# The first two units of a streamed trunk step divided at 256 tokens, and the first norm's root taken in token columns

## The chip, the core and the metric

One core of a Trainium2 chip runs the program. The metric is the device time of one execution in microseconds. All times in the profile are microseconds from the start of the span unless marked ns. The engines are TensorE (PE), VectorE (DVE), ScalarE (ACT), GpSimd (POOL) and SyncE (SP), which issues most DMAs; each executes its own list of instructions in order and waits on semaphores.

## What is computed

One layer of a hybrid trunk for 512 prompt tokens and 32 sample tokens, with all weights shared. Only the first half-step FFN and its norm are touched:

```
def rms_norm(x, g):
    y = xf * lax.rsqrt(jnp.mean(xf * xf, axis=-1, keepdims=True) + EPS)
    return (y * g.astype(jnp.float32)).astype(x.dtype)
def swiglu(x, wg, wu, wd):
    return (jax.nn.silu(x @ wg) * (x @ wu)) @ wd
# trunk_layer:
x = x + 0.5 * swiglu(rms_norm(x, g_ffn1), w_ffn1_gate, w_ffn1_up, w_ffn1_down)
... # mixer (mLSTM and retention), second half-step FFN
y_prompt = rms_norm(hp, g_final)
```

D_MODEL is 1024, D_FF 2816. Everything is float32.

## The kernel before

The 544 tokens (T) are kept as columns: x is turned to xT, 8 k-tiles (DT) of 128 features by 544 tokens. The token chunks are 0 to 3 of 128 tokens each, and the sample chunk, index NC = 4, of 32. A **unit** is one product of 128 output features with all tokens; units 0 and 1 are gate and up of the first 128 features of D_FF, units 2 and 3 of the next, and so on. Each product runs in a split form: weights and inputs are each divided into a rounded part (w_hi, xg_hi) and a rest (w_lo, xg_lo), and three of the four combinations are summed in PSUM: hi by hi ("hh"), hi by lo ("hl"), lo by hi ("lh"). A matmul takes TH = 272 columns, so a unit is 8 k-tiles x 3 parts x 2 halves = 48 matmuls.

At the start SyncE loads x chunk by chunk (x_tok, token rows) and the first weights (w_raw); the weights of unit 0 come in two halves of four k-tiles. TensorE first turns 12 dummies, then x (L848, L840) and the gains (L836) into PSUM. dense[0] and dense[1] hold one chunk each, so chunks 2 and 3 wait until 0 and 1 are copied out. VectorE copies most pieces to xT (L1779, L1782), ScalarE two of them (L1267). ScalarE makes xg_hi = gain times xT, 544 columns for each k-tile (L1042), and w_hi (L1272, L1284, L1030); VectorE makes xg_lo (L1424) and w_lo (L1784, L1790, L1419). The norm is not applied to xg but later, to the product: its factor rstd is multiplied in when a unit is evicted from PSUM (L1678, L1685).

For rstd, ScalarE squares x by token rows with a sum along the row (L1255, x_sums, one column for each chunk); GpSimd writes each sum on the diagonal of a block of sq_sum (L2065); TensorE multiplies it by a matrix of ones (L626, norm_sums_of), which puts each token's sum in its column on all partitions. In unit 1, behind its k-tile 5, these matmuls stand (SUMS_K). ScalarE takes the root over 544 columns (L1047) and VectorE the reciprocal (L1430).

The order of everything is the order in which each engine's part is written. The functions that matter are first_product (unit 0), second_product (unit 1) and plain (all other units of this kind) on TensorE, plain and the code ahead of ffn(0, 0) on ScalarE and VectorE, and spread_sums on GpSimd. Unit 2 needs w_lo of its own (w_lo_ready) and no eviction, since it writes to other banks; unit 3 needs unit 0 evicted, unit 4 unit 1.

## Time and profile before

| | us |
|---|---|
| median of 3 runs (1066.98 to 1067.19) | 1067.0 |
| the profiled execution | 1067.28 |
| its span, first to last instruction | 1065.5 |
| TensorE busy | 1055.8 (99%) |
| VectorE busy | 686.1 (64%) |
| ScalarE busy | 467.6 (44%) |
| GpSimd busy | 191.2 (18%) |

The profile is of one execution. The 1.8 us between its time and its span lie around the program. A share of busy time is an average; what a change is worth is read at the place where it is made, from what waits there and for whom. A matmul's record is longer than the step to the next, since they are pipelined: a row of n matmuls that takes t has steps of (t - one) / (n - 1). A releaser in brackets is inferred from the semaphores.

### The profile page before, as it was taken

Reading aid. Unit: us, or ns where it says so; the run is one execution under the profiler, and the core shown is the slowest. Engines: PE = TensorE matmul, PEld = TensorE weight load, DVE = VectorE, ACT = ScalarE, POOL = GpSimd, SP = SyncE. Lnnn points to the kernel's source line nnn. Section 1 sums busy time; section 2 is a strip of 40 time slices with the busy share of each in tenths; the row PEclk is TensorE's granted clock in tenths of the full one; section 3 lists DMA queues with packets and bytes.
Section 4 is the critical chain, followed back from the end, with each engine's and each line's share of the span. In section 5 each row is a group of like instructions: output and inputs, shape, how many; then the busy total and the mean of one; then the engine's idle time right before and its main releaser. Section 6 shows DMA issues by size and latency. Waiting matters only on the chain.

```text
span 1065.5 us, 20471 instructions
## 1 busy us (share of the span) xinstructions
PE 1055.8 (99%) x8424; PEld 1052.3 (99%) x8424; DVE 686.1 (64%) x1161; ACT 467.6 (44%) x820; POOL 191.2 (18%) x168
## 2 busy tenths in 40 slices
PE   8999999999999999999999999999999999999997
PEld 8999999999999999999999999999999999999997
DVE  5998752357766676555655556598875236777555
ACT  7466641246663335433222224446664114666323
POOL 1122100012201211210332222212210002220111
PEclk9999999999999999999999999999999999999999
DMA  7489572388833377445454224547958338882422
GB/s 224 90 185 203 112 183 84 102 161 175 175 83 92 72 131 144 70 69 79 72 80 73 68 78 61 140 91 170 205 109 187 91 90 163 177 176 55 120 75 84
DMA packets 245350, 127.84 MB, mean 120 GB/s; under 512 B 9181, under 2 KB 243717, under 8 KB 245129
## 3 DMA queue, kind: packets, MB, share of 16 engines
q1 hardware_dynamic: 206888, 106.79, 41.4%
q0 software_dynamic: 38288, 19.72, 14.6%
q8 instruction: 67, 1.10, 0.4%
q14 instruction: 27, 0.21, 0.1%
q10 hardware_dynamic: 80, 0.02, 0.0%
HBM read 123.22 MB, written 3.29 MB: 119 GB/s over the span
## 4 chain that ended last, share of the span: by engine, by line
PE 98%; DMA 1%; DVE 0%; ACT 0%; SPq 0%; issue 0%; ACTq 0%
PE dense L589 52%; PE dense L737 30%; PE core_banks L737 5%; PE core_banks L589 3%; PE core_banks L890 1%; PE core_banks L905 1%; PE dense L793 1%; PE core_banks L908 1%; PE core_banks L880 1%; DMA x_tok<-in_x_prompt 1%; PE dense L646 1%; PE dense L659 1%; PE core_banks L874 0%; PE core_banks L917 0%; PE core_banks L876 0%; PE core_banks L774 0%
## 5 line engine op out<-in xcount | busy, mean ns | idle before, releaser
L1419 DVE TENSOR_TENSOR w_lo<-w_raw,w_hi 128x1024 fp32r<-128x1024 f32 (+2 forms) x119 | 132.8, 1134 | 55.1 <-ACT w_hi L1030 55.0
L1030 ACT ACTIVATE w_hi<-w_raw 128x1024 fp32r<-128x1024 f32 (+2 forms) x119 | 106.3, 906 | 89.2 <-PE dense L589 81.0
L589 PE MATMUL dense<-h_hi,w_hi 128*128 128x272 f32 x684 | 142.4, 290 | 0.0
L589 PE MATMUL dense<-xg_hi,w_hi 128*128 128x272 f32 x672 | 142.2, 293 | 0.0
L589 PE MATMUL dense<-h_lo,w_hi 128*128 128x272 f32 x684 | 141.2, 287 | 0.0
L589 PE MATMUL dense<-h_hi,w_lo 128*128 128x272 f32 x684 | 140.9, 287 | 0.0
L589 PE MATMUL dense<-xg_lo,w_hi 128*128 128x272 f32 x672 | 138.9, 288 | 0.0
L589 PE MATMUL dense<-xg_hi,w_lo 128*128 128x272 f32 x672 | 138.8, 288 | 0.0
L737 PE MATMUL dense<-x_op_hi,w_lo 128*128 128x272 f32 x432 | 124.6, 289 | 0.0
L737 PE MATMUL dense<-x_op_hi,w_hi 128*128 128x272 f32 x432 | 124.5, 288 | 0.0
L737 PE MATMUL dense<-x_late_hi,w_lo 128*128 128x272 f32 x432 | 124.5, 288 | 0.0
L737 PE MATMUL dense<-x_late_hi,w_hi 128*128 128x272 f32 x432 | 124.3, 288 | 0.0
L737 PE MATMUL dense<-x_late_lo,w_hi 128*128 128x272 f32 x432 | 124.2, 287 | 0.0
L737 PE MATMUL dense<-x_op_lo,w_hi 128*128 128x272 f32 x432 | 124.0, 287 | 0.0
L1476 DVE TENSOR_TENSOR w_lo<-w_src,w_hi 128x512 fp32r<-128x512 f32 x126 | 85.8, 689 | 50.0 <-ACT w_hi L1078 49.8
L1733 DVE SCALAR_TENSOR_TENSOR xT<-dense,xT 128x544 f32<-128x544 f32 x38 | 27.5, 724 | 135.4 <-PE dense L589 135.3
L589 PEld LDWEIGHTS dense<-h_lo,w_hi 128*128 128x128 f32 x684 | 107.9, 188 | 0.0
L589 PEld LDWEIGHTS dense<-h_hi,w_lo 128*128 128x128 f32 x684 | 106.8, 188 | 0.0
L589 PEld LDWEIGHTS dense<-h_hi,w_hi 128*128 128x128 f32 x684 | 106.7, 188 | 0.1
L589 PEld LDWEIGHTS dense<-xg_lo,w_hi 128*128 128x128 f32 x672 | 105.8, 188 | 0.0
L589 PEld LDWEIGHTS dense<-xg_hi,w_lo 128*128 128x128 f32 x672 | 105.1, 188 | 0.0
L589 PEld LDWEIGHTS dense<-xg_hi,w_hi 128*128 128x128 f32 x672 | 104.7, 188 | 0.2
(333 smaller groups left out, 2217.3 us busy)
## 6 DMA issues: line engine op xcount, KB each, us to landing
w_src<-in_w_ffn_gate SPq DMA_DIRECT2D x90, 256.0 KB, 4.8
w_raw<-in_w_ffn_up SPq DMA_DIRECT2D x90, 256.0 KB, 3.9
w_raw<-in_w_in SPq DMA_DIRECT2D x32, 512.0 KB, 8.9
w_raw<-in_w_ffn_down SPq DMA_DIRECT2D x32, 384.0 KB, 4.1
w_raw<-in_w_ffn_down SPq DMA_DIRECT2D x32, 320.0 KB, 3.5
w_src<-in_w_ffn_gate POOLq DMA_DIRECT2D x36, 256.0 KB, 5.4
w_raw<-in_w_ffn_up POOLq DMA_DIRECT2D x36, 256.0 KB, 5.8
w_raw<-in_w_ffn_up SPq DMA_DIRECT2D x8, 512.0 KB, 5.0
```

Source lines behind the costliest of these rows:

```text
L589: last = nc.tensor.matmul(out[:, half, 0:TH], w[:, s % 4, k, :], x(kt)[:, half * TH:(half + 1) * TH], start=start and n == 0 and m == 0, s ...
L646: last = nc.tensor.matmul(bank_of(0)[:, half, 0:TH], w[:, 0, k, :], x(k)[:, half * TH:(half + 1) * TH], start=m == 0, stop=m == len(order) ...
L659: last = nc.tensor.matmul(bank_of(1)[:, half, 0:TH], w[:, 1, k, :], part(k)[:, half * TH:(half + 1) * TH], start=w is w_hi and k == 0 and ...
L737: last = nc.tensor.matmul(banks[BANK[o]], w[:, k, :], x[:, k, :], start=o in OPENS and k == 0 and m == 0, stop=k == KH - 1 and m == 2, ski ...
L793: last = nc.tensor.matmul(bank_of(t)[:, part, 0:cols.stop - cols.start], w[:, (s + u) % 4, kt - u * split, :], x[:, kt, cols], start=kt == ...
L880: nc.tensor.matmul(X[:, 3, CH[c]], p(h, 1, CH[c]), p(h, 0, CH[c]), start=True, stop=True)
L890: last = nc.tensor.matmul(X[:, b, o * V1:(o + 1) * V1], k_tail[:, c, :], v_tok[:, c, :], start=True, stop=True)
L905: last = nc.tensor.matmul(out, score_tail[:, block], v_tok[:, c, :], start=True, stop=c == 0)
L1030: nc.scalar.activation(w_hi[:, s % 4, 0:k_tiles(s), :], raw, ACT.Copy).then_inc(w_hi_ready, 1)
L1419: nc.vector.tensor_tensor(w_lo[:, s % 4, 0:nk, :], w_raw[:, s % RAW, 0:nk, :], w_hi[:, s % 4, 0:nk, :].bitcast(F32), ALU.subtract).then_in ...
L1476: nc.vector.tensor_tensor(block_of(w_lo, n, o), source(p % 2, o), block_of(w_hi, n, o).bitcast(F32), ALU.subtract)\
L1733: nc.vector.scalar_tensor_tensor(x, halves(tile), factor, x, ALU.mult, ALU.add).then_inc(evicted, 1)
```

## The change

- Units 0 and 1 are divided by tokens into EARLY (256, chunks 0 and 1) and LATE (288, chunks 2, 3 and the sample). first_units replaces first_product and second_product: unit 0 early, with the turns of the sample, chunk 2 and half of chunk 3 set between its products; unit 1 early (hh and hl), the last half of chunk 3, unit 1 early lh; then the late tokens of both units side by side. The matmuls have 256 and 288 columns. Both units are done at the same moment.
- Chunks 2 and 3 and the sample are turned into other PSUM banks (x_home) and no longer wait for dense. The eight dummies before the first product are gone.
- xg_hi and xg_lo of units 0 and 1 are made in 8 early and 8 late pieces. Unit 1's weights too come in two halves, unit 0's first half moves up to the third place in SyncE's list, before the sample.
- The first norm: GpSimd makes rstd itself, in one column for each chunk (mean and eps, then a power of -0.5), before it writes it on the diagonal. TensorE's matmuls then yield rstd in columns, and ScalarE only copies it. Reciprocal and root over 544 columns go. ScalarE squares chunks 0 and 1 ahead of the first product, the sample and chunk 2 behind the late pieces; VectorE squares chunk 3. The matmuls with ones move from unit 1 to unit 2, behind two of its k-tiles.

In the diff, cut to its core:

```diff
-    X_BY_ACT = [(2, 1), (3, 1)]
+    X_BY_ACT = [(2, 0), (2, 1)]
+    NA = 2 * P
+    EARLY, LATE = slice(0, NA), slice(NA, T)
...
+        def x_home(c, half):
+            if c < 2:
+                return dense[c][:, half, :]
+            if c == 2:
+                return X[:, half, :]
+            if c == NC:
+                return X[:, 2, 0:DT * TS]
+            return X[:, 3, :] if half == 0 else X[:, 0, :]
...
             load_x(0)
             load_x(1)
+            load_half(0, w_ffn1_gate, 0)
             load_x(NC)
             load_x(2)
+            load_half(0, w_ffn1_gate, 1)
             load_x(3)
+            load_half(1, w_ffn1_up, 0)
+            load_half(1, w_ffn1_up, 1)
...
-            SUMS_K = (5, 5, 6)
+            SUMS_K = (2, 5, 6)
...
+            def first_units():
+
+                order = [("hh", 0)]
+                for k in range(1, DT):
+                    order += [("hh", k), ("lh", k - 1), ("hl", k - 1)]
+                order += [("lh", DT - 1), ("hl", DT - 1)]
                 for m, (part, k) in enumerate(order):
+                    first_part(0, part, k, False, m == 0, m == len(order) - 1)
+                    if (part, k) == ("hl", 2):
+                        for piece in ((NC, 0), (2, 0), (2, 1)):
+                            turn_x(*piece)
+                    if (part, k) == ("hl", 4):
+                        turn_x(3, 0)
+                pe.wait_ge(x_taken, 4)
+                for k in range(DT):
+                    for part in ("hh", "hl"):
+                        first_part(1, part, k, False, part == "hh" and k == 0, False)
+                turn_x(3, 1)
+                for k in range(DT):
+                    first_part(1, "lh", k, False, False, k == DT - 1)
+                for m, (part, k) in enumerate(order):
+                    for u in range(2):
+                        last = first_part(u, part, k, True, m == 0, m == len(order) - 1)
...
-            turn_dummies(KEEP_WARM)
...
+                if n == 0:
+
+                    nc.scalar.activation(rstd[:, :].rearrange("p (a b) -> p a b", a=2), X[:, 0:2, 0:TH], ACT.Copy).then_inc(rstd_ready, 1)
+                    return
...
+                link(nc.gpsimd.tensor_scalar(col, x_sums[0:r, c:c + 1], 1.0 / D, EPS, ALU.mult, ALU.add))
+                link(nc.gpsimd.tensor_tensor(col, col, minus_half[0:r, c:c + 1], ALU.pow))
+                nc.gpsimd.tensor_scalar(sq_sum[0:r, CH[c]], ident[0:r, 0:r], col, None, ALU.mult).then_inc(x_sums_spread, 1)
+
+            for n, c in enumerate((0, 1, NC, NC - 1, 2)):
+                spread_rstd(n, c)
```

How instructions stand in a row, at three places. TensorE, from the turns of the sample on (dense0 and dense1 are the banks of units 0 and 1; core_banks, in the code X, are four others). Before:

```order
L840 MATMUL core_banks<-sum_ident,x_tok 128x32 x7
L836 MATMUL core_banks<-sum_ident,gain_rows 128x40 [waits gains_loaded]
L848 MATMUL dense<-sum_ident,x_tok 128x128 [waits x_taken,x_loaded2]
...
L848 MATMUL dense<-sum_ident,x_tok 128x128 [waits x_taken,x_end_loaded]
L848 MATMUL dense<-sum_ident,x_tok 128x128 x3
L829 MATMUL core_banks<-sum_ident 128x128 x8
L646 MATMUL dense<-xg_hi,w_hi 128x272 [waits half_hi,xg_hi_ready,x_taken_act,x_taken]
```

Now, from the gains on:

```order
L884 MATMUL core_banks<-sum_ident,gain_rows 128x40 [waits gains_loaded]
L668 MATMUL dense<-xg_hi,w_hi 128x256 [waits early_hi,half_hi0] x2
...
L668 MATMUL dense<-xg_lo,w_hi 128x256 [waits early_lo,half_hi0]
L873 MATMUL core_banks<-sum_ident,x_tok 128x32 [waits x_loaded4]
L873 MATMUL core_banks<-sum_ident,x_tok 128x32 x7
L877 MATMUL core_banks<-sum_ident,x_tok 128x128 [waits x_loaded2]
...
L668 MATMUL dense<-xg_lo,w_hi 128x256 [waits early_lo,w_hi_ready]
L877 MATMUL core_banks<-sum_ident,x_tok 128x128 [waits x_taken_act,x_end_loaded]
L877 MATMUL core_banks<-sum_ident,x_tok 128x128 x3
L668 MATMUL dense<-xg_hi,w_lo 128x256 [waits early_hi,half_lo1] x4
```

The first products stand ahead of the turns of the sample, and the last half of chunk 3 stands behind 40 of them.

ScalarE, from the gains to unit 2's weights. Before:

```order
L1261 ACTIVATE gains<-core_banks 128x40 [waits gains_moved]
L1267 ACTIVATE xT<-dense 128x4x128 [waits x_moved]
L1272 ACTIVATE w_hi<-w_raw 128x512 [waits half_loaded]
L1042 ACTIVATE xg_hi<-xT,gains 128x544 [waits gains_ready,x_taken]
...
L1030 ACTIVATE w_hi<-w_raw 128x1024 [waits w_loaded1]
L1255 ACTIVATE x_squared,x_sums<-x_tok 128x1024 [waits x_summed,x_end_loaded,x_loaded3]
L1030 ACTIVATE w_hi<-w_raw 128x1024 [waits w_loaded2]
```

Now:

```order
L1300 ACTIVATE w_hi<-w_raw 128x512 [waits half_loaded0]
L1313 ACTIVATE gains<-core_banks 128x40 [waits gains_moved]
L1317 ACTIVATE xg_hi<-xT,gains 128x256 [waits x_taken,gains_ready]
...
L1306 ACTIVATE xT<-core_banks 128x4x128 [waits x_moved] x2
L1328 ACTIVATE xg_hi<-xT,gains 128x288 [waits x_taken_act,x_taken] x8
L1063 ACTIVATE w_hi<-w_raw 128x1024 [waits w_loaded2]
L1294 ACTIVATE x_squared,x_sums<-x_tok 32x1024 [waits x_summed,x_loaded4]
L1294 ACTIVATE x_squared,x_sums<-x_tok 128x1024 [waits x_summed,x_loaded2]
L1063 ACTIVATE w_hi<-w_raw 128x1024 [waits w_loaded3]
```

Two squares now stand behind the late pieces and behind unit 2's weights.

GpSimd, behind its constants, the first chunk. Before:

```order
L2061 MEMSET sum_ident 128x544
L2065 TENSOR_SCALAR sum_ident<-sum_ident,x_sums 128x128 [waits x_summed,pool_step]
```

Now:

```order
L2138 MEMSET minus_half 128x5 [waits pool_step]
L2147 TENSOR_SCALAR x_rstd<-x_sums 128x1 [waits x_summed,pool_step]
L2148 TENSOR_TENSOR x_rstd<-x_rstd,minus_half 128x1 [waits pool_step]
L2149 TENSOR_SCALAR sum_ident<-sum_ident,x_rstd 128x128 [waits pool_step]
```

One operation for each chunk has become three, each waiting for the one before (pool_step); the five chunks follow each other so.

## Rows read from the trace of the kernel before

**Rows 1.** The page: the chain that ended last, share of the span by engine.
```profile
PE 98%; DMA 1%; DVE 0%; ACT 0%; SPq 0%; issue 0%; ACTq 0%
```
**Rows 2.** Waits of TensorE: who waited for whom, us in total, times, longest.
```profile
PE dense L804 <- ACT rms_bias L1220: 0.9, 1, 0.9
PE dense L848 <- DMA x_tok<-in_x_prompt: 0.6, 1, 0.6
PE dense L646 <- ACT xg_hi L1042: 0.4, 1, 0.4
```
**Rows 3.** Timeline of TensorE, start: start us, us, engine line op, xcount [idle before].
```profile
1.90 2.82 PE L829 MATMUL core_banks<-sum_ident 128*128 128x128 f32 x12 [1.90 <-POOL eps L2028]
...
7.35 0.68 PE L840 MATMUL core_banks<-sum_ident,x_tok 32*128 32x32 f32 x8
7.96 0.25 PE L836 MATMUL core_banks<-sum_ident,gain_rows 40*128 40x40 f32 x1
...
11.22 1.04 PE L829 MATMUL core_banks<-sum_ident 128*128 128x128 f32 x8
12.30 0.49 PE L646 MATMUL dense<-xg_hi,w_hi 128*128 128x272 f32 x2
...
13.43 0.49 PE L646 MATMUL dense<-xg_hi,w_hi 128*128 128x272 f32 x2 [0.39 <-ACT xg_hi L1042]
```
**Rows 4.** Timeline of TensorE, units 1 and 2, and the first matmul of unit 3.
```profile
22.31 0.41 PE L659 MATMUL dense<-xg_lo,w_hi 128*128 128x272 f32 x2
...
23.73 0.41 PE L659 MATMUL dense<-xg_lo,w_hi 128*128 128x272 f32 x2
...
24.48 2.17 PE L659 MATMUL dense<-xg_hi,w_lo 128*128 128x272 f32 x16
26.49 0.41 PE L589 MATMUL core_banks<-xg_hi,w_hi 128*128 128x272 f32 x2
...
32.52 0.29 PE L589 MATMUL dense<-xg_hi,w_hi 128*128 128x272 f32 x1
```
**Rows 5.** Timeline of ScalarE, 7 to 21 us.
```profile
7.14 1.06 ACT L1255 ACTIVATE x_squared<-x_tok 32x1024 f32<-32x1024 f32 x1
...
8.38 1.06 ACT L1255 ACTIVATE x_squared<-x_tok 128x1024 f32<-128x1024 f32 x1
...
10.00 0.63 ACT L1272 ACTIVATE w_hi<-w_raw 128x512 fp32r<-128x512 f32 x1
...
12.54 2.02 ACT L1042 ACTIVATE xg_hi<-xT,gains 128x544 fp32r<-128x544 f32 x3
...
19.54 1.04 ACT L1030 ACTIVATE w_hi<-w_raw 128x1024 fp32r<-128x1024 f32 x1
```
**Rows 6.** Timeline of VectorE, 6 to 16 us.
```profile
6.46 1.89 DVE L1779 COPY xT<-dense 128x512 f32<-128x512 f32 x3 [0.16 <-PE dense L848]
...
13.31 2.18 DVE L1424 SCALAR_TENSOR_TENSOR xg_lo<-xT,gains,xg_hi 128x544 fp32r<-128x544 f32 x3 [0.34 <-ACT xg_hi L1042]
```
**Rows 7.** DMA issues at 1.73, 2.19 and 4.83 us: xcount, KB each, us to landing.
```profile
x_tok<-in_x_sample SPq DMA_DIRECT2D x1, 128.0 KB, 4.7
...
x_tok<-in_x_prompt SPq DMA_DIRECT2D x1, 512.0 KB, 6.1
...
w_raw<-in_w_ffn_up SPq DMA_DIRECT2D x1, 512.0 KB, 8.6
```
**Rows 8.** Single lines L1042 and L1216 of ScalarE: xcount, ns min/median/max, first and last start.
```profile
L1042 ACT ACTIVATE xg_hi<-xT,gains x24: 734/750/755, 11.4 to 682.5; 128x544 fp32r<-128x544 f32 x24
...
L1216 ACT ACTIVATE x_gain<-xT,gains x2: 508/523/538, 1053.8 to 1058.4; 128x288 f32<-128x288 f32 x1, 128x256 f32<-128x256 f32 x1
```
**Rows 9.** GpSimd: its line L2065, its power L2112, and two small forms (xcount | busy, mean ns).
```profile
L2065 POOL TENSOR_SCALAR sum_ident<-sum_ident,x_sums x5: 354/605/770, 6.0 to 19.7; 128x128 f32<-128x128 f32 x4, 32x32 f32<-32x32 f32 x1
...
L2112 POOL TENSOR_TENSOR small<-small x8: 1168/1180/1202, 437.4 to 639.8; 128x5 f32<-128x5 f32 x8
...
L2106 POOL TENSOR_TENSOR sum_ident<-proj,table 128x32 f32<-128x32 f32 x4 | 1.0, 247 | 0.0
...
L2028 POOL MEMSET eps<- 128x1 f32 x1 | 0.1, 99 | 0.0
```

More of the change, by code:

```diff
@@ L650, in second_product, with first_part @@
[L650 to L663 removed]
+            def first_part(u, part, k, late, start, stop):
+                w, x = {"hh": (w_hi, xg[0]), "hl": (w_hi, xg[1]), "lh": (w_lo, xg[0])}[part]
+                half, cols = (1, LATE) if late else (0, EARLY)
+                if part == "lh":
+                    if k < DT // 2:
+                        pe.wait_ge(half_lo[u], 1)
+                    else:
+                        pe.wait_ge(w_lo_ready, u + 1)
+                elif k < DT // 2:
+                    pe.wait_ge(half_hi[u], 1)
+                else:
+                    pe.wait_ge(w_hi_ready, u + 1)
+                if part == "hl":
+                    pe.wait_ge(xg_lo_ready if late else early_lo, k + 1)
+                else:
+                    pe.wait_ge(xg_hi_ready if late else early_hi, k + 1)
+                a = 0 if late else 512 - NA
+                return nc.tensor.matmul(bank_of(u)[:, half, a:a + cols.stop - cols.start], w[:, u, k, :], x(k)[:, cols],
+                                        start=start, stop=stop)
@@ L1285, in _ @@
-            split_hi(0, 1, 0)
-            square_x(NC, NC - 1)
+            act.wait_ge(gains_ready, 1)
+            for j in range(DT):
+                act.wait_ge(x_taken, X_BY_DVE.index((1, 2 * j // DT)) + 1)
+                nc.scalar.activation(xg_hi[:, j, EARLY], xT[:, j, EARLY], ACT.Copy, scale=gains[:, G_FFN1 + j:G_FFN1 + j + 1])\
+                    .then_inc(early_hi, 1)
+                if j == DT // 2 - 1:
+                    half_to_hi(0, 1)
+            half_to_hi(1, 0)
+            half_to_hi(1, 1)
@@ L1288, in _ @@
+            for c, half in X_BY_ACT:
+                take_x(c, half)
+            for j in range(DT):
+                act.wait_ge(x_taken, X_BY_DVE.index((3, 2 * j // DT)) + 1)
+                act.wait_ge(x_taken_act, X_BY_ACT.index((2, 2 * j // DT)) + 1)
+                nc.scalar.activation(xg_hi[:, j, LATE], xT[:, j, LATE], ACT.Copy, scale=gains[:, G_FFN1 + j:G_FFN1 + j + 1])\
+                    .then_inc(xg_hi_ready, 1)
             ffn(0, 0)
@@ L1792, in _, with half_to_lo @@
-            split_lo(0, 1, 0)
+                    out, tiles = xT[:, :, CH[c]], x_home(c, half).rearrange("p (k d) -> p k d", d=TS)
+                nc.vector.tensor_copy(out, tiles).then_inc(x_taken, 1)
+            def half_to_lo(u, half):
+                k = slice(half * DT // 2, (half + 1) * DT // 2)
+                if half:
+                    dve.wait_ge(w_hi_ready, u + 1)
+                else:
+                    dve.wait_ge(half_hi[u], 1)
+                nc.vector.tensor_tensor(w_lo[:, u, k, :], w_raw[:, u, k, :], w_hi[:, u, k, :].bitcast(F32), ALU.subtract)\
+                    .then_inc(w_lo_ready if half else half_lo[u], 1)
@@ new lines, in part_lo @@
+            def part_lo(j, cols, hi_ready, lo_ready):
+                dve.wait_ge(hi_ready, j + 1)
+                nc.vector.scalar_tensor_tensor(xg_lo[:, j, cols], xT[:, j, cols], gains[:, G_FFN1 + j:G_FFN1 + j + 1],
+                                               xg_hi[:, j, cols].bitcast(F32), ALU.mult, ALU.subtract).then_inc(lo_ready, 1)
+            for c in range(2):
+                for half in range(2):
+                    take_x(c, half)
+            for j in range(DT):
+                if 2 * j % DT == 0:
+                    half_to_lo(0, 2 * j // DT)
+                part_lo(j, EARLY, early_hi, early_lo)
```

199 lines of the change are left out of this document (88 added, 111 removed).

## Prediction

> **What bounds the kernel now.** I read the page's chain first: TensorE carries 98% of it [rows 1]. Past the wait before its first instruction, the list of waits has three of TensorE: 0.6 for a piece of x, 0.4 for a piece of xg_hi, 0.9 in the tail [rows 2]. So what the change can move is what happens before TensorE's stream closes; from there on each microsecond saved or lost goes to the end unchanged. I then read TensorE's timeline of the start [rows 3]. Behind the turns of chunks 0 and 1 the sample rows are turned at 7.35, the gains at 7.96, then chunks 2 and 3 as their DMAs land; eight dummy transposes fill from 11.22; the first product starts at 12.30, and at 13.43 the second k-tile of xg_hi lets it go on. The two first units are through at 26.49, when unit 2 begins, and unit 3 begins at 32.52 [rows 4]. Within that, the norm's sums cost 0.92: from the pair of products at 22.31 to the one at 23.73 are 1.42, less two pairs at 0.25.
>
> **The sum is made at the start of unit 3**, because the norm's sums move from unit 1 into unit 2. Before: 32.52. Without its sums the first pair of units would have ended at 26.49 - 0.92 = 25.57.
>
> **When the first product starts now.** Chunks 0 and 1 are turned and copied as before: VectorE's fourth copy ends at 6.46 + 1.89 = 8.35 [rows 6]. ScalarE needs the gains before it can scale. They are turned on TensorE right behind chunk 1, where the sample rows began at 7.35, and no longer behind these, at 7.96 [rows 3]. No row says when their DMA landed, so these are the bounds; I take 7.7, the middle. ScalarE meanwhile does two squares, 1.24 from one to the next (7.14 to 8.38), and the first half of w_hi (0.63) [rows 5], whose DMA is now third instead of fifth in the queue: 1.25 MB into the stream, where the sample rows (1.125 MB) landed 4.7 us after issue at 1.73, that is 6.4, and chunk 2 (1.625 MB) at 2.19 + 6.1 = 8.3 [rows 7]. By that scale it lands at 6.9, ScalarE is through by 7.6. Gains: 7.7 + 0.25 for the turn, 0.18 for the copy, some 0.1 of hand-overs: 8.2. The first early piece of xg_hi is 256 columns wide, a form that the trace has: 508 ns [rows 8]. End 8.73, and TensorE starts 0.14 after such an end (13.43, after ScalarE's piece begun at 12.54, of three in 2.02, so 0.75 long and 0.64 a step [rows 5]). First product: **8.87**, bounds 8.5 and 9.15.
>
> **What TensorE does from there to unit 2.** The same columns as before in as many products, cut otherwise: 48 of 256 columns and 48 of 288 where 96 had 272. Those run 0.1253 apart (the row of 16 begun at 24.48: (2.17 - 0.29) / 15 [rows 4]); by columns that is 0.118 and 0.133, and the 96 keep their 12.03: cutting is free. Turning moves in between: 16 turns at (1.04 - 0.27) / 7 = 0.110, as the dummies', are 1.75, and the sample rows 0.70 [rows 3]. In the first groups the pieces come at ScalarE's and VectorE's pace (some 0.41 each for 256 columns: the 0.64 a step less 288 columns at (750 - 508) / 288 = 0.84 ns), and TensorE asks for three products, 0.35, per piece: three small waits of 0.2 in all, and 0.35 where a group's first matmul follows a wait (0.20 to the second in place of 0.125, as at 13.43). Weight halves come in time: w_hi's second at 9.95 + 0.6, those of unit 1 when 2.875 and 3.125 MB are in (12.5 and 13.4; the whole landed at 4.83 + 8.6 = 13.4 before), split by 14.1 [rows 5, 7], and TensorE is at unit 1 at 14.3. If a weight half were 0.5 late, that cover would be gone and it would cost about that. Sum: 8.87 + 12.03 + 2.45 + 0.55 = 23.9, **23.95** with its last matmul's hand-over, for the start of unit 2: 1.6 earlier than 25.57. Removing the eight dummies costs nothing by itself: they stood in a wait.
>
> **The norm's sums are what is late next.** They stand after two of unit 2's eight k-tiles: 12 matmuls, so TensorE asks for all five diagonal blocks at 23.95 + 1.50 = 25.45, and as its queue is in order, everything behind waits: 36 more products of unit 2 and all that follows. What must be done by then:
> - TensorE reaches the last piece of chunk 3 only behind unit 1's 16 products: 8.87 + 0.55 + 40 x 0.118 + 2.0 of turns = 16.15. It ends its four turns at 16.85, and VectorE has copied it by 17.5 (1.89 for three such copies, some 0.65 [rows 6]).
> - ScalarE's late pieces 4 to 7 wait for that copy. A 288-column piece takes 538 ns [rows 8], 0.44 a step, so the four steps end at 19.3. Then it splits w_hi of unit 2 (1.04), to 20.3, squares the sample rows, to 21.5, and chunk 2, to 22.7 (1.24 each) [rows 5]. The order rows in the section on the change show this row of instructions; before, these two squares lay ahead of the first product.
> - VectorE: eight late lo pieces to 21.0 (0.44 a step: three of 544 columns took 2.18, 0.70 a step [rows 6], less 256 columns at 1.0 ns, its time per column by the same row), then chunk 3's square over 1024 columns, some 1.2: 22.2. Unit 2's w_lo, as many columns, then ends at 23.3, ahead of 23.95 by 0.65. The reciprocal of the first norm leaves VectorE and brings nothing: TensorE did not wait for it [rows 2].
> - GpSimd now does three operations for each chunk in place of one, and chunks sample, 3 and 2 still lie ahead of it at 21.5. The wide one is 354 to 770 ns by its row; I take 0.35 for the sample and 0.77 for the others, the latest and longest of the five [rows 9]. The scale and shift of one column: between a 128x1 memset, 0.10, and the 32x32 form, 0.354; I take 0.27. The power of one column: the nearest row is the power of 128x5, 1.18 us; the nearest without a power is a product of 128x32, 0.247. If the 0.93 between them is work per column, one column costs 0.25 + 0.19 = 0.44. Three self-waits are some 0.06 each. The chain is then 21.5 + 1.26 = 22.76, + 1.66 = 24.4, + 1.66 = **26.1**, 0.15 more to TensorE: it starts the sums at 26.25, 0.8 late.
>
> **Sum.** -1.6 + 0.8 = -0.8 at the start of unit 3 (31.7). Behind it I see nothing that becomes late: the root's copy and the first eviction, each some 0.75 for 544 columns [rows 5, 6], need some 1.7 us with hand-overs, and TensorE has 4.5 us of unit 2 left; the second eviction has 6 us more. The table load before the root goes; the one for the silu stays behind the copy, off TensorE's path. The profiled execution would have a span of 1064.7 and, with the 1.8 around it, 1066.5; that run stood 0.3 above the median of 1067.0, so the forecast is 1067.0 - 0.8 = **1066.2**.
>
> What a page says of this, outside the sum: the Trainium skill, "GPSIMD Engine Reference", section "Elementwise — side-by-side cycle accounting", counts about 2.6 cycles per element and a dispatch for each instruction, so a power of one column would cost little more than the start of an instruction. The row [rows 9] speaks against taking that for powers: five columns cost 1.18 us where 32 columns of a product cost 0.247. By the page's rule the stall would be 0.2 and the time 1065.6.
>
> **The rivals.**
> - *The power has a fixed price (slower).* If one column costs what five cost, 1.18, the three powers in a row add 3 x 0.74 = 2.2 to the chain: blocks ready at 28.3, TensorE idle for 3.0, net +1.4: 1068.4. The point is a power of 0.71: 0.8 of gain is then eaten. For it: the row is the only power in the trace, and its eight instances lie within 3%. Against: a product of 544 columns on GpSimd takes far longer than one of 32, so its operations are counted per column.
> - *No stall at the sums.* With 0.25 for the power and 0.10 for the scale the blocks are ready at 25.0: the whole 1.6 stays, 1065.4; with the gains' DMA at its early bound, 1065.0.
> - *TensorE's pace falls back.* The granted clock reads 1.00 from the start, yet the first twelve transposes stand 0.218 apart ((2.82 - 0.42) / 11) and the later dummies 0.110 [rows 3]: half the pace, in TensorE's first microseconds.  Now it is nearly idle from 7.3 to 8.9 with no dummies behind. If it came back for some 4.4 us (the dummies' 2.6 and as much of chunk 0), 2.2 us would be lost: +1.4, 1068.4. Against it: it is 1.6 us of idling, and the trace has waits of 0.6 and 0.4 [rows 2] with no loss of pace behind them. "TensorE: Matmul & The Clock Gate" of the Trainium skill, section "Part 1: The HAM clock gate (the "warmup" mystery)", says that half pace is the default and that an idle engine returns to it; by it the price would be the same.
> - *The change does not fill the gap.* The early tokens come no sooner if the gains or the first weight half land later than I scaled; 0.5 later moves the whole start by 0.5 and leaves 1066.7, inside the main case.
>
> **How the numbers follow.** Main case (power near 0.44, stall 0.3 to 1.3) 0.50, 1065.7 to 1066.9; fixed price 0.22; no stall 0.15; pace 0.05; the rest 0.08, of it half each way. The range reaches from the no-stall case with early gains, 1065.0, to the fixed-price case, 1068.5. A difference of 0.2%, 2.1 us, is about what a measurement of this kernel can tell from none. Faster by more would need over 2.1 of the 3 us that lay open before the first product, without any stall: 0.05. Slower by more needs the fixed price and the pace together, or a late DMA on top of one: 0.06. Within: 0.89.
>
> **What would show it.** In the profile after: the first product of 256 columns near 8.9; unit 2's first near 23.9; an idle of TensorE just before the sums' matmuls, released by GpSimd, of about 0.8; one power on GpSimd near 0.44. A power near 1.2, or transposes 0.21 apart after 8 us, would name the rival. No wait at all and a gain of 1.6 would mean the small operations are cheaper than I hold. Wrong altogether if unit 3 waits for the first eviction, or if TensorE waits at unit 2 for w_lo.

## The result, and the profile after

The change made the kernel slower. The median went from 1066.99 us (6 runs, 1066.8 to 1067.35) to 1072.18 us (6 runs, 1071.37 to 1075.63), a ratio of 1.0048 with a 95% interval of 1.0034 to 1.0062. The profiled run of after took 1071.62 us with a span of 1069.9, against 1067.28 and 1065.5 before: 4.4 us more between the first and the last instruction. Three runs far off all others (one at 1280 us in experiment 9, and two of before beside it, at 1134 and 2130) count in no comparison below.

All of it is there when unit 3 begins, at 36.86 us against 32.52 [rows 4], 4.34 later. Four views show from where. First the waits of TensorE in the profile after (who waited for whom, us in total, times, longest), to be read against [rows 2]:

```profile
PE core_banks L647 <- POOL sum_ident L2149: 2.7, 1, 2.7
...
PE dense L668 <- ACT xg_hi L1317: 0.9, 1, 0.9
...
PE core_banks L884 <- DMA gain_rows<-in_g_gn_ret: 0.5, 1, 0.5
```

The wait for GpSimd at the norm's sums was forecast, at 0.8. It is 2.7. Then TensorE's timeline (start us, us, what, xcount, [idle before]), which answers to [rows 3, 4]:

```profile
7.70 0.25 PE L884 MATMUL core_banks<-sum_ident,gain_rows 40*128 40x40 f32 x1 [0.54 <-DMA gain_rows<-in_g_gn_ret]
8.89 0.83 PE L668 MATMUL dense<-xg_hi,w_hi 128*128 128x256 f32 x2 [0.94 <-ACT xg_hi L1317]
...
10.02 0.41 PE L668 MATMUL dense<-xg_hi,w_hi 128*128 128x256 f32 x1
10.23 0.41 PE L668 MATMUL dense<-xg_hi,w_lo 128*128 128x256 f32 x1
10.44 0.41 PE L668 MATMUL dense<-xg_lo,w_hi 128*128 128x256 f32 x1
...
12.42 1.97 PE L877 MATMUL core_banks<-sum_ident,x_tok 128*128 128x128 f32 x8
...
16.64 0.28 PE L668 MATMUL dense<-xg_hi,w_hi 128*128 128x256 f32 x1
16.76 0.28 PE L668 MATMUL dense<-xg_hi,w_lo 128*128 128x256 f32 x1
...
26.90 0.42 PE L616 MATMUL core_banks<-xg_hi,w_hi 128*128 128x272 f32 x2
...
28.16 0.42 PE L616 MATMUL core_banks<-xg_hi,w_lo 128*128 128x272 f32 x2
31.31 1.19 PE L647 MATMUL core_banks<-sum_ident,ones 128*128 128x272 f32 x4 [2.73 <-POOL sum_ident L2149]
...
36.86 0.41 PE L616 MATMUL dense<-xg_hi,w_hi 128*128 128x272 f32 x2
```

The first product starts at 8.89, in place of 12.30. But from there to 16 us the products of 256 columns start 0.21 apart (10.02, 10.23, 10.44) and eight turns take 1.97, where behind 16.6 us the same products are 0.12 apart. TensorE's granted clock in stretches of 2 us (the columns are the stretch, busy time and instructions of PE, its weight loads, VectorE, ScalarE and GpSimd, then the granted clock, the DMA share and GB/s) says the same:

```profile
8.00:10.00 2.00, 1.06 (x4) 0.92 (x5) 2.00 (x5) 1.97 (x7) 1.22 (x2) 0.86 1.07 349
10.00:12.00 2.00, 2.00 (x14) 1.78 (x12) 2.00 (x6) 2.00 (x5) 0.00 (x0) 0.50 1.15 309
12.00:14.00 2.00, 2.00 (x13) 1.94 (x13) 1.11 (x3) 1.72 (x4) 0.00 (x0) 0.50 1.19 291
14.00:16.00 2.00, 2.00 (x11) 2.00 (x10) 0.00 (x0) 0.76 (x2) 0.00 (x0) 0.50 1.07 224
16.00:18.00 2.00, 2.00 (x18) 2.00 (x17) 1.51 (x3) 0.78 (x2) 0.00 (x0) 0.94 0.75 193
```

0.50 is the lower of the two levels, 1.2 GHz in place of 2.4. It lasts from 9.5 to 16.3 us, and it begins after TensorE stood idle for 0.54 and 0.94 us with one transpose between. In before every such stretch up to 36 us reads 1.00. Unit 2 therefore starts at 26.90 and not at the forecast 23.95. "TensorE: Matmul & The Clock Gate" of the Trainium skill, section "Part 1: The HAM clock gate (the "warmup" mystery)", names the lower level as the engine's default when idle. The trace agrees on the two levels, and shows the fall behind two idle stretches as short as 0.54 and 0.94 us.

The other part is GpSimd's chain. Its timeline, with one power of chunk 1 first, then the three operations for the sample and those for chunk 3, and under it VectorE's timeline over the same time:

```profile
7.92 0.58 POOL L2148 TENSOR_TENSOR x_rstd<-x_rstd,minus_half 128x1 f32<-128x1 f32 x1
...
24.39 0.68 POOL L2147 TENSOR_SCALAR x_rstd<-x_sums 32x1 f32<-32x1 f32 x1 [15.08 <-ACT x_squared L1294]
25.16 1.44 POOL L2148 TENSOR_TENSOR x_rstd<-x_rstd,minus_half 32x1 f32<-32x1 f32 x1
26.70 1.29 POOL L2149 TENSOR_SCALAR sum_ident<-sum_ident,x_rstd 32x32 f32<-32x32 f32 x1
28.08 0.19 POOL L2147 TENSOR_SCALAR x_rstd<-x_sums 128x1 f32<-128x1 f32 x1
28.35 0.57 POOL L2148 TENSOR_TENSOR x_rstd<-x_rstd,minus_half 128x1 f32<-128x1 f32 x1
29.02 0.61 POOL L2149 TENSOR_SCALAR sum_ident<-sum_ident,x_rstd 128x128 f32<-128x128 f32 x1
```

```profile
23.82 1.22 DVE L1867 SCALAR_TENSOR_TENSOR x_squared_dve<-x_tok 128x1024 f32<-128x1024 f32 x1
...
24.96 1.22 DVE L1462 TENSOR_TENSOR w_lo<-w_raw,w_hi 128x1024 fp32r<-128x1024 f32 x1
26.54 1.23 DVE L1462 TENSOR_TENSOR w_lo<-w_raw,w_hi 128x1024 fp32r<-128x1024 f32 x1 [0.36 <-ACT w_hi L1063]
```

The smallest of the five blocks is the slowest: 0.68, 1.44 and 1.29 us on 32 partitions, where the larger chunk 3 takes 0.19, 0.57 and 0.61. Each of the three slow ones ends just behind a VectorE instruction that was already running when it started: the first at 25.07 (VectorE's square ends at 25.04), the power at 26.60 (the first w_lo ends at 26.18), the scaling at 27.99 (the second ends at 27.77). Behind the last w_lo, VectorE is idle and GpSimd is quick.

### The profile page after: what moved, and what is told of

Read it like the earlier page. It is cut to its first block, busy times and chain, and to the rows that moved or that the text cites. A ratio compares the mean times of both kernels' runs of the same rounds, so it can differ in the third digit from the quotient of the medians.

```text
span 1069.9 us, 20574 instructions
## 1 busy us (share of the span) xinstructions
PE 1057.2 (99%) x8416; PEld 1054.2 (99%) x8416; DVE 685.0 (64%) x1171; ACT 467.1 (44%) x826; POOL 197.2 (18%) x179
## 4 chain that ended last, share of the span: by engine, by line
PE 97%; POOL 1%; ACT 1%; DMA 1%; DVE 0%; issue 0%; SPq 0%; ACTq 0%
PE dense L616 52%; PE dense L766 30%; PE core_banks L766 5%; PE core_banks L616 3%; PE core_banks L923 1%; PE core_banks L938 1%; PE dense L822 1%; PE core_banks L941 1%; PE core_banks L913 1%; PE dense L668 1%; DMA w_raw<-in_w_ffn_gate 1%; PE core_banks L950 0%; PE core_banks L909 0%; PE core_banks L907 0%; PE core_banks L647 0%; PE core_banks L877 0%
```

## The experiments

All edits are on after, except where before is named. Each set of experiments (1 to 4; 5 to 8; 9 and 10) had runs of before beside it, whose median was 1067.17, 1067.0 and 1067.03. Mean clocks are those of a whole run; half pace for 6.8 of 1065 us takes 0.003 off them.

**1. Fill TensorE's idle time.** Is it half pace that puts unit 2 three us late?

```diff
+            turn_dummies(5)
             pe.wait_ge(gains_loaded, 16 * 6)
             nc.tensor.transpose(X[:, 3, 0:5 * DT], gain_rows[:, :], ...)
+            turn_dummies(8)
             ffn(0, 0)
```

> The kernel after with 13 more dummy transposes of TensorE: 5 ahead of the gains' turn and 8 behind it, where it stood idle from 7.2 to 7.7 and from 7.95 to 8.9. Theory: two things ate the gain, TensorE's half pace from 9.3 to 16.1 us (products of 256 columns 0.213 apart instead of 0.118), which came after that idling, and the wait of 2.7 us before the norm's sums. Then the half pace is gone: products 0.118 apart from the first on, unit 2 at 23.95 as predicted instead of 26.90, the wait before the sums as long as it was (ScalarE's squares and GpSimd's blocks move with TensorE), time 1072.2 - 2.9 = 1069.3. Rival: the half pace comes from the mixture of short products and turns with their waits, not from the idling; then it stays and so does 1072.2.

Measured: median 1069.3 (1068.67 to 1072.31, 6 runs), ratio to before 1.0026 (1.0015 to 1.0038): the forecast value. Every stretch from 8 to 28 us reads 1.00, unit 2 starts at 24.80. That is 0.85 behind the expectation, as the first product is (9.74), for two reasons: chunk 1's turns ended later, and the five dummies ahead of the gains' turn then stood in no wait, so that they delayed it by some 0.5 themselves (experiment 5, with as late a chunk 1 and no dummies, has 9.07). The profiled run was the slowest, 1072.31, and shows why: half pace now came later, behind the wait at the sums. In the views of TensorE's timeline and of the stretches:

```profile
29.19 2.18 PE L647 MATMUL core_banks<-sum_ident,ones 128*128 128x272 f32 x4 [2.71 <-POOL sum_ident L2151]
```

```profile
28.00:30.00 2.00, 0.81 (x2) 0.69 (x3) 0.00 (x0) 0.00 (x0) 1.04 (x2) 0.60 1.06 305
30.00:32.00 2.00, 2.00 (x8) 1.64 (x7) 0.00 (x0) 0.59 (x1) 0.00 (x0) 0.50 1.09 282
```

So the dummies take half pace out of the start, and the wait at the sums can bring it back. Of the six runs four lie at 1068.7 to 1069.4 and two above 1071.

**2. Ask for the sums later**, behind six k-tiles of unit 2.

```diff
-            SUMS_K = (2, 5, 6)
+            SUMS_K = (6, 5, 6)
```

> The kernel after with the matmuls of the norm's sums behind six of unit 2's eight k-tiles instead of two (24 matmuls, 3.0 us later in TensorE's order). Theory: the wait of 2.7 to 2.9 us before the sums is one for GpSimd's blocks, which come when they come; TensorE works 3.0 us of unit 2 meanwhile, so the wait goes but for 0.1, and what is left of unit 2 (12 matmuls, 1.5 us) just covers root copy and eviction: 1072.2 - 2.8 = 1069.4. Rival: the wait only moves to unit 3, which then waits for unit 0's eviction: over 1071. The half pace at the start stays in both.

Measured: median 1072.1 (1068.31 to 1072.98, 7 runs), ratio 1.0036 (1.0022 to 1.005). The wait at the sums is gone (they start at 32.28, the last block was ready at 32.09), and the median is that of after. In the profiled run the first product came 0.8 later than in after, because the first weight half landed later. Behind unit 3, which starts at 34.92, two waits on VectorE and ScalarE stand that after does not have. The timeline of TensorE:

```profile
9.72 0.76 PE L668 MATMUL dense<-xg_hi,w_hi 128*128 128x256 f32 x2 [1.71 <-ACT xg_hi L1317]
...
41.60 0.52 PE L616 MATMUL dense<-xg_hi,w_hi 128*128 128x272 f32 x2 [0.41 <-DVE w_lo L1462]
...
70.27 0.39 PE L766 MATMUL dense<-x_op_hi,w_hi 128*128 128x272 f32 x1 [1.28 <-ACT kept L1136]
```

With steps of 0.125 as normal, the step to 41.60 (0.70) loses 0.6, that to 70.27 (1.56) loses 1.4, and one at 34.92 (0.34) loses 0.2: 2.2 in all. After has no such step behind 32.5. So of the 2.7 us 2.2 were given back, and the late first product took more than the rest. That the later root is what made ScalarE and VectorE late is my reading of the order; no run tests it. Two of the seven runs, at 1068.31 and 1068.63, have mean clocks of 0.999 and 0.998 against 0.994 to 0.996 of four others: without half pace the kernel lies just below the 1068.7 to 1069.4 of experiment 1, which again leaves a gain of some 0.5 of the 2.7. (The seventh, 1072.98 at 0.999, is not explained.) My expectation, 1069.4, missed the new waits.

**3. Square earlier.** ScalarE's squares of the sample and of chunk 2 go between its late pieces 3 and 4, where it waited for chunk 3; VectorE's square of chunk 3 goes ahead of the last copy of x.

```diff
-                        square_x(2, NC)
-                        square_x(3, 2)
...
             for j in range(DT):
+                if j == DT // 2:
+                    square_x(2, NC)
+                    square_x(3, 2)
...
             half_to_lo(1, 1)
-            take_x(3, 1)
-            for j in range(DT):
-                part_lo(j, LATE, xg_hi_ready, xg_lo_ready)
...
+            take_x(3, 1)
+            for j in range(DT):
+                part_lo(j, LATE, xg_hi_ready, xg_lo_ready)
```

> The kernel after with the three late squares moved ahead: ScalarE's of the sample rows and of chunk 2 into its idle time between late pieces 3 and 4, VectorE's of chunk 3 into its idle time ahead of the copy of the last half of chunk 3. Theory: the blocks are then ready before TensorE asks for them at 28.4, the wait is gone, and the late pieces of xg_hi lose nothing since TensorE is at unit 1's early products: 1072.2 - 2.9 = 1069.3. Rival: the late pieces 4 to 7 slip by up to 1.0 and TensorE waits for them: 1070.3 or more. Also tells why GpSimd's first chain took 0.68, 1.44 and 1.29 us where the next took 0.19, 0.57 and 0.61: if VectorE's split of weights beside it is the cause, the sample's chain is short now; if the first chain after a long idle time is slow by itself, it is as long as before.

Measured: median 1068.16 (1065.32 to 1070.01, 10 runs), ratio 1.0006 (0.9994 to 1.0017). The wait at the sums is gone, although the profiled run (1069.82) has half pace from 10.5 to 17.3 us, as long as after has. The four runs at 1065.3 to 1065.9, with mean clocks of 0.998 and 0.999, are below every run of before; the six at 1067.5 to 1070.0 have 0.994 to 0.997. In the profiled run the gains landed late, so that the first product came 1.3 later than in after:

```profile
9.03 0.25 PE L884 MATMUL core_banks<-sum_ident,gain_rows 40*128 40x40 f32 x1 [1.35 <-DMA gain_rows<-in_g_gn_ret]
10.21 0.95 PE L668 MATMUL dense<-xg_hi,w_hi 128*128 128x256 f32 x2 [0.92 <-ACT xg_hi L1315]
```

GpSimd's timeline and VectorE's, here with other neighbours:

```profile
21.64 0.56 POOL L2149 TENSOR_TENSOR x_rstd<-x_rstd,minus_half 32x1 f32<-32x1 f32 x1
22.30 0.50 POOL L2150 TENSOR_SCALAR sum_ident<-sum_ident,x_rstd 32x32 f32<-32x32 f32 x1
...
26.59 1.43 POOL L2149 TENSOR_TENSOR x_rstd<-x_rstd,minus_half 128x1 f32<-128x1 f32 x1
```

```profile
25.23 2.36 DVE L1463 TENSOR_TENSOR w_lo<-w_raw,w_hi 128x1024 fp32r<-128x1024 f32 x2
```

The sample's power is quick now, 0.56, and that of chunk 2, beside w_lo, takes 1.43. So neither 32 partitions nor being the first after a long idle makes an operation slow; the company of VectorE does. The edit moves all three squares at once, so what each is worth was not told apart.

**4. Before, without its eight dummies**, for the prediction's statement that removing them costs nothing.

```diff
-            turn_dummies(KEEP_WARM)
             ffn(0, 0)
```

> The kernel before without its eight dummy transposes between the turns of x and the first product (11.2 to 12.3 us). Theory: the dummies are what kept TensorE's pace there; without them idle time from 11.4 to 12.3 and at 13.0 brings the half pace back for about as long as in the kernel after, 6.8 us, which costs 3: 1070. Rival: the idle time of 0.9 us is too short to matter, everything is as before: 1067.0.

Measured: median 1066.94 (1066.79 to 1070.15, 10 runs), ratio 1.0003 (0.9994 to 1.0013). TensorE then idles for 0.92 us before its first product at 11.97, and the profiled run stays at full clock. Eight of the ten runs lie within 1066.8 to 1067.6; two, at 1069.7 and 1070.15, have the size of a loss that half pace brings, but their mean clock is 0.999, where after's six runs have 0.992 to 0.996. So half pace does not show in them, and what cost the 3 us stays open.

**5. Hold one w_lo of VectorE** until GpSimd is through, to test the standing side by side alone.

```diff
                     if n == 0 and u == 0:
+                        dve.wait_ge(x_sums_spread, NC + 1)
                         split_lo(0, s + 3, 0)
```

> After, with one wait more: VectorE's split of unit 3's w_lo (1.22 us, begun at 26.54) waits until GpSimd has written all five blocks. Unit 2's split, begun at 24.96, stays. Theory (GpSimd and VectorE exclude one another during such an instruction): the sample's scaling on GpSimd, which took 1.29 beside that split, takes about 0.6, while its power beside unit 2's split stays at 1.44; the blocks are ready 0.7 earlier, the wait at the sums is 2.0 in place of 2.7, the time 1071.5. Rival (first operations after a long idle, or operations on 32 partitions, are slow by themselves): scaling stays at 1.29, wait 2.7, 1072.2.

Measured: median 1069.77 (1067.75 to 1073.24, 7 runs), ratio 1.0032 (1.0019 to 1.0044). GpSimd's timeline, the sample's power and scaling and the last scaling, and the first product and the wait at the sums on TensorE's:

```profile
25.61 1.44 POOL L2149 TENSOR_TENSOR x_rstd<-x_rstd,minus_half 32x1 f32<-32x1 f32 x1
27.14 0.36 POOL L2150 TENSOR_SCALAR sum_ident<-sum_ident,x_rstd 32x32 f32<-32x32 f32 x1
...
30.16 0.61 POOL L2150 TENSOR_SCALAR sum_ident<-sum_ident,x_rstd 128x128 f32<-128x128 f32 x1
```

```profile
9.07 0.76 PE L668 MATMUL dense<-xg_hi,w_hi 128*128 128x256 f32 x2 [0.93 <-ACT xg_hi L1317]
...
30.82 1.49 PE L647 MATMUL core_banks<-sum_ident,ones 128*128 128x272 f32 x4 [1.78 <-POOL sum_ident L2150]
```

The one operation whose neighbour was taken away fell from 1.29 to 0.36; the one beside the w_lo that stayed kept its 1.44. From the chain's first start to its last end it is 5.93 (24.84 to 30.77) in place of 6.86 (24.39 to 31.25), and the wait went from 2.73 to 1.78. That settles the cause of the long chain: VectorE's company, and neither the 32 partitions nor the idle time ahead. This profiled run had only one idle stretch at its start, 0.93 before the first product at 9.07, and fell to 0.50 all the same, from 11.1 us. In the medians the clock's scatter is larger than the effect tested, so the verdict rests on the rows.

**6. Dummies and squares together**, the diffs of 1 and 3 in one kernel.

> After with both edits of the earlier runs: five dummy turns ahead of the gains' and eight behind it, and the squares moved forward (ScalarE's sample and chunk 2 between late pieces 3 and 4, VectorE's chunk 3 ahead of the last copy of x). Theory (two causes, half pace after the start and a late chain on GpSimd): the run with squares moved gave 1065.3 to 1065.9 where its clock did not fall, so now every run should stand there, 1065.5 in the median, with unit 2 at 24.3 to 24.9 us, no half pace before 30 us and a wait at the sums under 0.7. Rival (TensorE comes early and GpSimd does not follow, since its chain starts behind ScalarE's squares and VectorE's splits whatever the clock is): a wait at the sums of over 1.5 and 1067 or more, and half pace behind that wait in some runs.

Measured: median 1066.2 (1065.39 to 1071.16, 11 runs), ratio 0.9994 (0.9986 to 1.0003). Ten of the eleven runs lie at 1065.4 to 1066.5, one at 1071.2. The profile has no wait at the sums and no clock below 1.00 up to 36 us:

```profile
8.86 0.76 PE L668 MATMUL dense<-xg_hi,w_hi 128*128 128x256 f32 x2
...
23.92 0.42 PE L616 MATMUL core_banks<-xg_hi,w_hi 128*128 128x272 f32 x2
...
25.43 1.08 PE L647 MATMUL core_banks<-sum_ident,ones 128*128 128x272 f32 x4
...
30.86 0.41 PE L616 MATMUL dense<-xg_hi,w_hi 128*128 128x272 f32 x2
```

Unit 3 starts at 30.86, 1.66 before that of before, and the span is 1063.9, 1.6 shorter. The last block was ready at 24.77, so 0.66 was to spare. Against before the medians alone do not settle a gain, since the interval holds 1.0; that the start is 1.66 shorter rests on the rows.

**7. The same, and unit 3's w_lo held** as in 5.

> As the kernel with both edits, and VectorE's split of unit 3's w_lo waits for all five blocks of rstd from GpSimd. Theory (a GpSimd operation stands still until VectorE's subtraction of two SBUF operands ends): the last operations on GpSimd take their 0.19, 0.57 and 0.61 and the blocks are ready up to 1.0 us earlier than without the hold; the time is equal or up to 0.7 lower, 1065.0 to 1065.5. Rival (GpSimd is slow for a reason of its own): no operation of it gets shorter, same time. If unit 3's weights then come late for unit 3, a wait of TensorE for w_lo appears at about 31 us and the time is higher.

Measured: median 1065.76 (1065.37 to 1068.48, 11 runs), ratio 0.9991 (0.9982 to 1.0). The power of chunk 2, the last in the chain, takes 0.57 (1.43 in 6), its scaling 0.61, and the last block is ready at 23.95, 0.8 earlier. Nothing waited for that any more, and unit 3's weights were not late. The profiled span is 1063.6, shorter than in 6 by 0.3, of which 0.25 is the earlier first product (8.61). So the hold shortened the chain and bought no time, and the lower median, 0.4 under that of 6, is not shown to come from it. This is the fastest of all the kernels, 1.2 us under before; its interval reaches just up to 1.0.

**8. Before, with the norm part of the change alone** (GpSimd's three operations, ScalarE's copy, no reciprocal).

```diff
-            spread_sums(n, c)
+            spread_rstd(n, c)
...
+                if n == 0:
+                    nc.scalar.activation(rstd[...], X[:, 0:2, 0:TH], ACT.Copy).then_inc(rstd_ready, 1)
+                    return
```

> Before, with the norm part of the change alone: GpSimd raises to -0.5 in one column for each chunk and writes that on the diagonal, ScalarE copies instead of taking the root, VectorE takes no reciprocal; the units, the dummies and the place of the sums are those of before. Theory (the norm part is cheap where its chain has room): the last block is ready at 19.7 + 0.27 + 0.66 + 0.77 = 21.4 or, if VectorE's split of two SBUF operands lies beside it, up to 1 us later, the sums are asked at 22.6: 1067.0, within 0.3 of before. Rival (the norm part itself is what costs): a wait of TensorE at the sums, over 1067.5.

Measured: median 1067.13 (1066.84 to 1069.04, 10 runs), ratio 1.0002 (0.9993 to 1.0011). No wait at the sums. The last scaling, beside a w_lo, takes 1.50 in place of 0.61:

```profile
20.42 1.50 POOL L2077 TENSOR_SCALAR sum_ident<-sum_ident,x_rstd 128x128 f32<-128x128 f32 x1
```

It ends at 21.92, 0.25 ahead of the sums, at 22.17. The norm part is free where its chain has room.

**9. Which of the two idle stretches?** Dummies behind the gains' turn only (eight), and ahead of it only (five).

```diff
             nc.tensor.transpose(X[:, 3, 0:5 * DT], gain_rows[:, :], ...)
+            turn_dummies(8)
             ffn(0, 0)
```

> After, with the eight dummy turns behind the gains' turn alone (none ahead). Idle left: from the end of chunk 1's turns to the gains, 0.5 us in the profiled run of after and up to 1.4 by when the gains land. Theory (half pace follows when TensorE's idling between 7 and 9 us adds up to nearly 1 us or more): no half pace where the gains land early, since 0.5 alone is left; where they land late there is. Most runs like those with all thirteen dummies: a wait of 2.7 at the sums, 1069.3; unit 2 at 24 to 25 us in the profile. Rival (any idle there at all is enough): unit 2 at 26.9 and 1072.

Measured: median 1068.92 of the nine runs that count, which lie at 1068.7 to 1071.6 (1069.25 with the tenth, 1280), ratio 1.0023 (1.0013 to 1.0033). Profile: the clock stays at 1.00, one idle of 0.55 is left, unit 2 at 24.13, a wait of 2.72 at the sums, span 1067.1.

The other kernel:

```diff
+            turn_dummies(5)
             pe.wait_ge(gains_loaded, 16 * 6)
```

> After, with the five dummy turns ahead of the gains' turn alone (none behind). Idle left: 0.93 from the gains to the first product, as in the profile of the run with unit 3's split held, which fell to half pace at 10.5 us with just that. Theory: half pace from about 10 us, unit 2 near 27 us, 1072. Rival (it takes both gaps, 1.5 us): unit 2 at 24 to 25, 1069.3.

Measured: median 1069.89 (1068.63 to 1072.28, 10 runs), ratio 1.0027 (1.0017 to 1.0037). Profile: idle of 0.86 and 1.41, because the gains and then the first weight half landed late (the fall of experiment 5, with 0.93 alone, was at 11.1 us and not at 10.5); the first product at 9.80, unit 2 at 26.41. Here half pace began later than in after, at about 12 us, and lasted 3.4 us in place of 6.8: from the first product to unit 2 are 16.6, where 15.1 is the time without it and 18.0 that of after. In the view of the stretches:

```profile
10.00:12.00 2.00, 1.95 (x17) 1.70 (x17) 1.96 (x5) 2.00 (x6) 0.00 (x0) 0.99 1.17 308
12.00:14.00 2.00, 2.00 (x13) 1.94 (x11) 2.00 (x6) 1.68 (x5) 0.00 (x0) 0.50 1.11 273
14.00:16.00 2.00, 2.00 (x14) 2.00 (x13) 0.04 (x2) 1.53 (x3) 0.00 (x0) 0.66 0.84 222
```

Half of the runs, five of ten, are at 1068.6 to 1069.4, as if it had not come. Neither expectation was met cleanly: with either stretch left open it comes in some executions and not in others. With the filler behind the gains six of nine runs are at 1068.7 to 1069.6, with the one ahead five of ten, too close to rank the two stretches.

**10. Before, with an idle of that length put in.**

```diff
             for c, half in X_PIECES:
+                if (c, half) == (NC, 0):
+                    pe.wait_ge(x_taken, 4)
```

> Before, with one wait more on TensorE: the turns of the sample wait until VectorE has copied chunk 1's second half, which makes TensorE idle from about 7.3 to 8.4 us. Nothing else changes, and TensorE has dummies to spare until 12.3. Theory (an idle of about 1 us that early brings half pace for some 7 us, whatever the kernel around it): transposes 0.21 apart from about 9.5 us, products of 272 columns 0.23 apart until 16 us, the first product later by up to 1 and the whole 1069 to 1070. Rival (the change's new order of products and turns, or their lower activity, is needed for it): no half pace, 1067.0.

Measured: median 1067.44 (1067.17 to 1070.07, 10 runs), ratio 1.0005 (0.9996 to 1.0015). TensorE's timeline:

```profile
8.40 0.68 PE L842 MATMUL core_banks<-sum_ident,x_tok 32*128 32x32 f32 x8 [1.04 <-DVE xT L1781]
```

It idles 1.04 us, longer than the single 0.93 of experiment 5, and the clock stays at 1.00. One run of ten is 2.6 above the median; its mean clock is 0.995 and that of the other nine 0.998, so there half pace probably came. My theory, that an idle of about 1 us so early always brings half pace, is wrong. What decides, beside the length of the idle, stays open.

## Why the prediction was wrong

It said 1066.2, within 1065.0 to 1068.5; the time was 1072.18. The profile splits the difference in two, a start at half pace and a chain of GpSimd that lasted longer than I had it. Unit 3 was forecast at 31.7 and began at 36.86, 5.15 later: 2.95 is the start of unit 2, and nearly all the rest the wait at the sums, 2.9 from its asking (28.16 + 0.25 = 28.41) to 31.31 in place of 0.8.

- **The first product, right.** Forecast 8.87, measured 8.89. The gains' turn stood at the middle I took, 7.70. That both fit so closely is in part luck. In the profiles of the eight kernels with the changed start of experiments 1 to 3, 5 to 7 and 9 the first product lies between 8.61 and 10.21, and in four of them beyond my bound of 9.15: the gains or the first weight half landed later, and in experiment 1 chunk 1's turns and the dummies behind them ended later. In the four profiles with before's start it lay at 11.91 to 12.38. I had named this as a rival ("The change does not fill the gap"), priced 0.5 of lateness at 0.5, and left out that a late landing also makes TensorE idle longer: three of those four fell to half pace (experiments 2, 3 and the second kernel of 9).
- **Work up to unit 2, right in its terms and wrong in their pace.** The sum said that unit 2 starts at 23.95. In the run of experiment 6, where the clock stayed up, it started at 23.92 from a first product at 8.86. The products of 256 and 288 columns are 0.118 and 0.133 apart, as cut by columns. The first step that failed is "TensorE's pace falls back": it had a chance of 0.05 and a price of 2.2 us. It came, with a price of 2.95, and in after's six runs none came near the times without it. I had argued against it with waits of 0.6 and 0.4 that cost no pace [rows 2], while I myself had counted 1.6 us of near idling here. A row that shows a shorter idle without a loss does not speak about a longer one. The removal of the dummies was costed on the same ground, at nothing, and in before it is nothing (experiment 4: 1066.94). In the changed kernel the idle time lies elsewhere, just behind the turns of chunk 1.
- **The wait at the sums, right mechanism and mis-sized chain.** I had the chain of GpSimd begin 2.45 ahead of unit 2 (21.5 against 23.95); it began 2.5 ahead (24.39 against 26.90). I had it last 4.6 us; it lasted 6.86. Its own operations were forecast well in sum: a power 0.57 in place of 0.44, so three powers cost 0.4 more, a scale and shift 0.19 in place of 0.27, a wide scaling 0.61 in place of 0.77. The excess is the sample's: 0.68 less 0.19, 1.44 less 0.57 and 1.29 less 0.36 are 2.3 us, in which GpSimd stood still beside three VectorE instructions that read two operands from SBUF. The second step that failed is that I let GpSimd run freely from 21.5, at nothing for its neighbour. I had listed VectorE's square, ending at 22.2, and unit 2's w_lo, ending at 23.3, in that very stretch, and had not put one beside the other; the third, unit 3's w_lo, I had not listed at all. The trace of before had the hint. Of the four operations of one form, 128x128, that [rows 9] puts at a median of 0.605, three take 0.60 to 0.62 and the last 0.77. GpSimd's timeline of before, and VectorE's beside it:

```profile
9.62 0.60 POOL L2065 TENSOR_SCALAR sum_ident<-sum_ident,x_sums 128x128 f32<-128x128 f32 x1 [0.89 <-ACT x_squared L1255]
19.72 0.77 POOL L2065 TENSOR_SCALAR sum_ident<-sum_ident,x_sums 128x128 f32<-128x128 f32 x1 [9.49 <-ACT x_squared L1255]
```

```profile
18.80 1.22 DVE L1419 TENSOR_TENSOR w_lo<-w_raw,w_hi 128x1024 fp32r<-128x1024 f32 x1
```

The 0.77 starts within that w_lo, which ends at 20.02, and ends 0.47 behind it. I used it as the length of a late operation without asking why it was longer.
- **The fixed price of a power** was the rival I had given 0.22. It is false: one column costs 0.57, five cost 1.18 [rows 9]. Its time, 1068.4, would have been right in size for the wait (3.0 against 2.9) for the wrong reason.
- **The first term of the sum stands.** With both causes taken away unit 3 is 1.66 earlier, against the 1.6 that I forecast ahead of any wait. That the median there is the forecast's 1066.2 is luck: my sum had 0.8 of wait in it, which experiment 6 does not have, and its profiled span is 1063.9 against a forecast of 1064.7.
- **The parts of the norm** cost nothing by themselves, as said (experiment 8, where the chain has room). "Nothing becomes late behind it" held for after, but experiment 2 shows how narrow: asked for 4 k-tiles later, the sums bring 2.2 us of new waits.

Neither cause was in a term that I added up: one is TensorE's own pace, the other the company that VectorE keeps GpSimd. The range left them out together: 2.95 + 2.1 on top of 1066.2 are 1071.3. Of the remaining 0.9, 0.56 is the distance of the profiled run from the median above it, and 0.28 that of before's profiled run from the median below it.

On the second cause the Trainium skill, "SBUF — State Buffer", section "Who interferes with whom", says that a VectorE instruction with two SBUF inputs contends with a GpSimd instruction that reads SBUF, for ports that they share under an exclusive lock, and that the order of issue decides which of them blocks. The traces agree: the powers of 1.44 and 1.43 end 0.42 to 0.43 behind the end of the w_lo beside them. With the 2.3 us of excess that the runs show for it, the forecast wait of 0.8 becomes 3.1, where 2.9 was measured.

## What to carry to other kernels

When work on GpSimd stands on the path, lay VectorE's row of instructions beside it and count every operation that starts within a long VectorE instruction with two SBUF operands as ending only behind it; where there is room, let VectorE do that work before or after the chain. An idle of TensorE that is counted as free waiting can have a second price when it comes behind the first short burst of work (3 us here, in some executions and not in others): fill it with dummy turns, which cost nothing while the engine waits anyway and their own length where it does not (0.5 us in experiment 1), and look at the granted clock in short stretches, not at the mean of 0.996. A wait that is moved out of one place should be followed to the places that depend on its result: here the sums asked for later gave back 2.2 us of the 2.7. And a start that is moved forward into the first DMAs takes over their scatter: the first product came between 8.6 and 10.2 us, where with the old slack it came between 11.9 and 12.4.

## What the runs showed of the hardware that I had not expected

- GpSimd's operations on one column: 0.56 to 0.58 us for a power, 0.18 to 0.19 for a scale and shift, 0.60 to 0.61 for a 128x128 scaling and 0.36 for 32x32, when VectorE leaves it alone. Beside VectorE's 1.22 us subtraction a power took up to 1.44, a scale and shift 1.28, a scaling 1.50 (128x128) and 1.29 (32x32). Whatever its kind, an operation that was caught so ended behind VectorE's by its own undisturbed time less 0.13 to 0.16: the powers 0.42 and 0.43 behind, the 128x128 scalings 0.46 and 0.47, the 32x32 one 0.22, the scale and shift beside the square 0.03. Beside the 288-column pieces of xg_lo (0.43 apart) a power took 0.65 to 0.72 and a 128x128 scaling 0.81 to 1.16.
- TensorE's granted clock fell to 0.50 behind these idle stretches in the profiles with the changed start: 0.54 and 0.94 (after), 1.71 (experiment 2), 1.35 and 0.92 (3), 0.93 (5), 0.86 and 1.41 (9, second kernel). It stayed at 1.00 behind 0.53 (6), 0.33 (7), 0.55 (9, first kernel) and none (1). In kernels with before's order it stayed at 1.00 behind 1.04 (10) and 0.92 (4). It began between 9.5 and 12.0 us and lasted 6.8 us in all but one of them, and in after it put unit 2 2.95 us late. A wait of 2.7 us at the sums was followed by it in experiment 1 and not in after or experiment 9; a wait of 1.78 was in experiment 5 (0.50 from 31.6 to 35.0 us).
- So one kernel has two or three times: experiment 3 gave 1065.3 to 1065.9 in four runs and 1067.5 to 1070.0 in six, where before's runs beside it lie within 1.1 us. A median of six runs of such a kernel says less than its profile.
